# Delta rule in a fused two-block kernel: where the z columns stand, and where their gate meets the normed outputs

## The reference

```python
h = rms_norm(x, norm_mix[i])
proj = h @ w_in[i]
qkv_a, qkv_b, z_b, beta_b, alpha_b, gate_a, gate_b = split_columns(proj, IN_WIDTHS)
...                                   # windowed attention -> o_a (512 wide)
qkv_b = causal_short_conv(qkv_b, conv_w[i])
...                                   # q, k, v of 8 heads x 128
o_b = gated_delta_rule(qb, kb, vb, beta, g)
o_b = rms_norm(o_b, dn_out_norm[i]) * jax.nn.silu(z_b.reshape(b, s, DN_HEADS, DN_HEAD_DIM))
merged = (jax.nn.sigmoid(gate_a) * (o_a @ w_branch_a[i])
          + jax.nn.sigmoid(gate_b) * (o_b @ w_branch_b[i]))
x = x + merged @ w_out[i]
...                                   # mixture of experts, then a last gated path
```

## Time and profile before

| | us |
|---|---|
| median of three runs | 3188.21 (3187.32 to 3191.43) |
| the profiled execution, its own time | 3185.6 |
| its span | 3183.8 |
| TensorE busy | 2901.0 (91%) |
| VectorE busy | 1703.5 (54%) |
| ScalarE busy | 1253.5 (39%) |

### The profile page before, as it was taken

The page is one execution under the profiler, slowest core; times in us unless marked ns, Lnnn a source line. Parts: engine busy times, 40 slices in busy tenths (PEclk is TensorE's granted clock), DMA queues, the critical chain, the costliest instruction groups (busy, mean ns, idle before and its releaser), DMA issues.

```text
span 3183.8 us, 35407 instructions
## 1 busy us (share of the span) xinstructions
PE 2901.0 (91%) x13998; PEld 2293.4 (72%) x13998; DVE 1703.5 (54%) x2469; ACT 1253.5 (39%) x1913; POOL 14.8 (0%) x22
## 2 busy tenths in 40 slices
PE   6998899999999988999999999997778789969997
PEld 5566677888886656777888887775467677858886
DVE  4455535555334565355554335457575545459995
ACT  3233233333221442234332224454535434348883
POOL 0000000000000000000000000000000000000000
PEclk9999899999999989999999999998889899979998
DMA  4111113233331112122333321111110102259981
GB/s 161 47 40 62 42 39 98 94 99 98 93 124 61 44 47 60 34 78 93 98 99 112 100 93 59 61 60 40 40 47 29 44 28 86 94 209 369 394 336 54
DMA packets 96180, 307.70 MB, mean 97 GB/s; under 512 B 25744, under 2 KB 31760, under 8 KB 84240
## 3 DMA queue, kind: packets, MB, share of 16 engines
q1 hardware_dynamic: 69056, 284.88, 26.3%
q10 hardware_dynamic: 24368, 11.12, 1.2%
q0 software_dynamic: 2592, 9.44, 0.8%
HBM read 296.49 MB, written 8.91 MB: 96 GB/s over the span
## 4 chain that ended last, share of the span: by engine, by line
PE 78%; DVE 10%; ACT 6%; issue 4%; DMA 1%; ACTq 1%; POOL 0%; POOLq 0%; DVEq 0%
PE bank L370 19%; PE bank L372 18%; PE bank L371 18%; PE bank L365 2%; PE bank L367 2%; PE bank L366 2%; ACT flow_head L389 2%; DVE flow_rest L400 1%; PE bank L1929 1%; DVE dn L1812 1%; PE bank L2526 1%; PE bank L1232 1%; PE bank L1066 1%; PE bank L559 1%; PE bank L2011 0%
## 5 line engine op out<-in xcount | busy, mean ns | idle before, releaser
L400 DVE TENSOR_TENSOR flow_rest<-flow_raw,flow_head 128x1024 fp32r<-128x1024 f32 (+2 forms) x372 | 438.5, 1179 | 940.6 <-ACT flow_head L389 940.6
L370 PE MATMUL bank<-h_head,flow_head 128*128 128x512 f32 x2144 | 899.1, 419 | 28.5 <-DVE flow_rest L400 24.1
L371 PE MATMUL bank<-h_rest,flow_head 128*128 128x512 f32 x2144 | 847.3, 395 | 0.0
L372 PE MATMUL bank<-h_head,flow_rest 128*128 128x512 f32 x2144 | 846.6, 395 | 0.0
L389 ACT ACTIVATE flow_head<-flow_raw 128x1024 fp32r<-128x1024 f32 (+2 forms) x372 | 379.2, 1020 | 734.6 <-PE bank L372 686.6
L370 PEld LDWEIGHTS bank<-h_head,flow_head 128*128 128x128 f32 x2144 | 411.3, 192 | 148.2 <-issue 60.6
L371 PEld LDWEIGHTS bank<-h_rest,flow_head 128*128 128x128 f32 x2144 | 410.9, 192 | 91.9 <-issue 16.2
L372 PEld LDWEIGHTS bank<-h_head,flow_rest 128*128 128x128 f32 x2144 | 409.1, 191 | 88.7
L372 PE MATMUL bank<-ff_head,flow_rest 128*128 128x512 f32 x352 | 137.1, 390 | 0.0
L371 PE MATMUL bank<-ff_rest,flow_head 128*128 128x512 f32 x352 | 137.1, 389 | 0.0
L370 PE MATMUL bank<-ff_head,flow_head 128*128 128x512 f32 x352 | 137.1, 389 | 0.0
(11 more groups left out here) (607 smaller groups left out, 4218.4 us busy)
## 6 DMA issues: line engine op xcount, KB each, us to landing
flow_raw<-in_w_in SPq DMA_DIRECT2D x176, 512.0 KB, 3.5
ring<-in_experts SPq DMA_DIRECT2D x84, 1024.0 KB, 7.7
flow_raw<-in_w_gate_up SPq DMA_DIRECT2D x88, 512.0 KB, 3.4
flow_raw<-in_w_down SPq DMA_DIRECT2D x32, 512.0 KB, 3.5
flow_raw<-in_w_out SPq DMA_DIRECT2D x24, 512.0 KB, 3.5
flow_raw<-in_paths SPq DMA_DIRECT2D x24, 256.0 KB, 2.6
flow_raw<-in_w_down SPq DMA_DIRECT2D x16, 384.0 KB, 3.1
flow_raw<-in_path_b SPq DMA_DIRECT2D x8, 512.0 KB, 3.5
```

The lines of the kernel that those rows point to most:

```text
L370: nc.tensor.matmul(ps[u.bank][:, :], wh[:, c:c + P], head, start=start, stop=False)
L371: nc.tensor.matmul(ps[u.bank][:, :], wh[:, c:c + P], rest, start=False, stop=False)
L372: last = nc.tensor.matmul(ps[u.bank][:, :], wr[:, c:c + P], head, start=False, stop=stop)
L400: nc.vector.tensor_tensor(self.parts_of[p.slot][1][:, 0:p.words], p.raw, f32(self.parts_of[p.slot][0][:, 0:p.words]), ALU.subtract).then_i ...
```

## The change

The z units stand where they stood in the flow, between path A and path B, with the same weights and the same 64 ticks. What changes is what is written around them. `ends[5]`, the t1 of the delta rule's second half, is now the end of the z units plus 2 ticks. So that half's stages are spread over the 96 ticks of path A and the 64 of z, all its fractions unchanged. The z units use banks 6 and 7 alone, since the delta rule uses 4 and 5; they keep tanh-gated z in a buffer of their own (`k.zg`, 8 chunks, where path A's operands were). The product with the normed outputs, its head and its rest are a step of their own, `gated_outputs`, written behind the second half's last norm: 8 products (L1915), 8 heads (L1929), 8 rests (L1922), one chunk per tick from 3 ticks after the z units' end. The number and shape of instructions stay the same, but for table loads. From L1908 on, the lines of the changed kernel are other ones, those from `unit_norm` to `mixer_2` stand 20 lines later.

```diff
-    k.zt = at("zt", 40, (2, S))
+    k.zg = at("z_gate", 20, (DC, S))
...
-        o = k.x[c // PART][0][:, c % PART, :]
-
-        def keep(v, m, q=q):
-            return nc.vector.tensor_tensor(k.zt[:, q, :], k.ps[flow.units[m].bank][:, :], k.root[:, :], ALU.mult)
+        z = k.zg[:, c, :]
+
+        def keep(v, m, z=z):
+            return nc.vector.tensor_tensor(z, k.ps[flow.units[m].bank][:, :], k.root[:, :], ALU.mult)
...
-            k.dve_chain(nc.vector.scalar_tensor_tensor(k.zt[:, q, :], k.sgf2[:, q, :], 1.0, k.zt[:, q, :], ALU.add, ALU.mult))
+            nc.vector.scalar_tensor_tensor(z, k.sgf2[:, q, :], 1.0, z, ALU.add, ALU.mult).then_inc(*k.z_ready.up())
+
+        m = flow.unit(6 + c % 2, [(p, r * P) for r in range(DC)], operand(False), [(1, keep), (3, gate)], [(2, squash)])
+    return m
+
+
+def gated_outputs(k, chunks, t0):
+
+
+    nc, flow, v, a = k.nc, k.flow, k.v, k.a
+    base = chunks[0]
+
+    def vector_part():
+        for c in chunks:
+            flow.dve(t0 + c - base)
+            v.wait_ge(*k.z_ready.at(c + 1))
             v.wait_ge(*k.out_normed.at(c + 1))
-            nc.vector.tensor_tensor(k.zt[:, q, :], k.zt[:, q, :], o, ALU.mult).then_inc(*k.z_gated.up())
+            nc.vector.tensor_tensor(k.zg[:, c, :], k.zg[:, c, :], k.x[c // PART][0][:, c % PART, :], ALU.mult).then_inc(*k.z_gated.up())
+            if c > base:
+                rest(c - 1)
+        rest(chunks[-1])
+
+    def rest(c):
+        v.wait_ge(*k.z_heads.at(c + 1))
+        nc.vector.scalar_tensor_tensor(k.dr[:, c, :], k.zg[:, c, :], 0.5, f32(k.dh[:, c, :]), ALU.mult,
+                                       ALU.subtract).then_inc(*k.dn_split.up())
+
+    def scalar_part():
+        for c in chunks:
+            flow.act(t0 + c - base)
             a.wait_ge(*k.z_gated.at(c + 1))
...
-    flow.unit(4 + c % 4, [(p, r * P) for r in range(DC)], operand(False), [(1, keep), (3, gate), (6, rests)],
-                  [(2, squash), (4, heads)])
+            nc.scalar.activation(k.dh[:, c, :], k.zg[:, c, :], ACT.Copy, scale=0.5).then_inc(*k.z_heads.up())
...
-    z_units(k, dram)
+    k.z_end = z_units(k, dram)
...
-    ends.append(flow.units[k.path_a_end].end + 2)
+    ends.append(flow.units[k.z_end].end + 2)
...
+    gated_outputs(k, range(DC), ends[5] + 1)
```

More of the change, by code:

```diff
@@ L1885, in z_units, with squash @@
         p, q = flow.piece(dram["w_in_2"][Z_UNIT + c]), c % 2
-        o = k.x[c // PART][0][:, c % PART, :]
-        def keep(v, m, q=q):
-            return nc.vector.tensor_tensor(k.zt[:, q, :], k.ps[flow.units[m].bank][:, :], k.root[:, :], ALU.mult)
-        def squash(a, m, q=q):
+        z = k.zg[:, c, :]
+        def keep(v, m, z=z):
+            return nc.vector.tensor_tensor(z, k.ps[flow.units[m].bank][:, :], k.root[:, :], ALU.mult)
+        def squash(a, m, q=q, z=z):
             k.tables(EXP_TANH)
@@ L1893, in squash, with gate @@
             a.wait_ge(*flow.emptied_by(m))
-            nc.scalar.activation(k.sgf2[:, q, :], k.zt[:, q, :], ACT.Tanh, scale=0.5).then_inc(*k.z_squashed.up())
-        def gate(v, m, c=c, q=q, o=o):
+            nc.scalar.activation(k.sgf2[:, q, :], z, ACT.Tanh, scale=0.5).then_inc(*k.z_squashed.up())
+        def gate(v, m, c=c, q=q, z=z):
             v.wait_ge(*k.z_squashed.at(c + 1))
-            k.dve_chain(nc.vector.scalar_tensor_tensor(k.zt[:, q, :], k.sgf2[:, q, :], 1.0, k.zt[:, q, :], ALU.add, ALU.mult))
-            v.wait_ge(*k.out_normed.at(c + 1))
-            nc.vector.tensor_tensor(k.zt[:, q, :], k.zt[:, q, :], o, ALU.mult).then_inc(*k.z_gated.up())
@@ L1902, in heads @@
-        def heads(a, m, c=c, q=q):
-            a.wait_ge(*k.z_gated.at(c + 1))
-            nc.scalar.activation(k.dh[:, c, :], k.zt[:, q, :], ACT.Copy, scale=0.5).then_inc(*k.z_heads.up())
-        def rests(v, m, c=c, q=q):
-            v.wait_ge(*k.z_heads.at(c + 1))
-            nc.vector.scalar_tensor_tensor(k.dr[:, c, :], k.zt[:, q, :], 0.5, f32(k.dh[:, c, :]), ALU.mult,
-                                           ALU.subtract).then_inc(*k.dn_split.up())
-        flow.unit(4 + c % 4, [(p, r * P) for r in range(DC)], operand(False), [(1, keep), (3, gate), (6, rests)],
-                  [(2, squash), (4, heads)])
+            nc.vector.scalar_tensor_tensor(z, k.sgf2[:, q, :], 1.0, z, ALU.add, ALU.mult).then_inc(*k.z_ready.up())
@@ new lines, in z_units @@
+        m = flow.unit(6 + c % 2, [(p, r * P) for r in range(DC)], operand(False), [(1, keep), (3, gate)], [(2, squash)])
[7 more added lines that the diff above has]
+            v.wait_ge(*k.z_ready.at(c + 1))
+            v.wait_ge(*k.out_normed.at(c + 1))
+            nc.vector.tensor_tensor(k.zg[:, c, :], k.zg[:, c, :], k.x[c // PART][0][:, c % PART, :], ALU.mult).then_inc(*k.z_gated.up())
[9 more added lines that the diff above has]
+            flow.act(t0 + c - base)
+            a.wait_ge(*k.z_gated.at(c + 1))
+            nc.scalar.activation(k.dh[:, c, :], k.zg[:, c, :], ACT.Copy, scale=0.5).then_inc(*k.z_heads.up())
+    vector_part()
+    scalar_part()
@@ L3405, in stream @@
             "conv_tapped", "conv_convolved", "conv_squashed", "conv_done", "gates_squashed_2", "paths_added_2", "merged_heads_2",
-            "merged_rests_2", "z_squashed", "z_gated", "z_heads", "attn_split", "dn_split", "table_2_landed", "qk_done",
+            "merged_rests_2", "z_squashed", "z_ready", "z_gated", "z_heads", "attn_split", "dn_split", "table_2_landed", "qk_done",
             "win_done", "gates_ready", "dn_normed", "out_normed"))
```

2 lines of the change are left out of this document (1 added, 1 removed).

## The result

The changed kernel takes 3202.37 us (median of 7 runs, 3193.86 to 3205.41) against 3187.32 (7 runs, 3181.58 to 3194.48) of the kernel before: ratio 1.0041, 95% interval 1.0029 to 1.0054. By the ratio that is 13 us slower, with 9 and 17 as bounds; the two medians are 15 apart. The time lies in the forecast range of 3186 to 3205, 6 us above the forecast time and 2.6 under the range's upper end.

What follows compares the result with a forecast made beforehand. TensorE, busy for 91% of the span, was taken to bound the kernel, with its idle time in the second half open to filling. Terms 1.8 + 1.0 - 3.8 + 9.2 = 8.2 us slower than 3188.2 gave 3196.4; range 3186 to 3205.

Steps and rivals of the forecast that it cites:

- q and k norm: Second half's norm before the pairs: 8 more ticks, but last Ln 7.2 us later through four more loads; 1.8 us lost.
- pairs: Matmuls after the q and k norm: said to wait for nothing themselves, before or after the change.
- block solve: Solve ahead of the inverse: one wait becomes 3.6, 2.3 and 6.9 us; 1.0 us lost (0.3 gained to 2 lost).
- inverse, scan, output norm: Rest of the second half: shorter waits and less low clock, against one new wait; 3.8 us gained.
- new step: Gated outputs before path B: waits of 2.0 and 5.5 us, next piece late, low clock; 9.2 us lost.
- set 1: First set of the inverse: a rest stands ahead of an update, giving a new wait of 1.4 us.
- set 2: Second set of the inverse: 3 ticks instead of 1 cut 1.4 us off the wait of 3.0.
- low clock behind the 3.0: Slow matmuls after the wait before the inverse's second set: 1.8 us lost before the change, which should go.
- Rival 4: Much slower: every table load costs double in both norms, 8 more loads than before; 3207 us, chance 0.04.
- Rival 3: Faster: other engines' chains keep their length, so each wait is cut by all its new ticks; 3179 us, chance 0.09.

Runs made afterwards that it cites:

- tables_qk: Changed kernel with the Ln and Exp table set asked for by name only in the second half's q and k norm; 3189.17 us.
- early_norm: Changed kernel with the second half of the delta rule ending 24 ticks earlier, the gated products left where they were; 3209.84 us.
- head_first: Changed kernel with the second half's first eight block solve DMA issues written one tick later, behind the flow head; 3195.00 us.
- tables_end6: Changed kernel with table set asked for in all norms, block solve's DMA issues one tick later, half's end 6 ticks earlier, products unmoved; 3166.39 us.
- before_tables: Kernel before the change with the table set asked for ahead of every Ln and Exp of the norms; 3167.89 us.
- split: Changed kernel with chunks 0 to 3 of the gated outputs moved ahead of the output norm; 3206.87 us.
- tables_out: Changed kernel with the Ln and Exp table set asked for by name only in the second half's output norm; 3195.11 us.
- tables: Changed kernel with the table set asked for ahead of every Ln and Exp of the norms; 3169.98 us.
- end_alone: Changed kernel with the delta rule's second half spread over path A only, gated products still behind the z units; 3192.35 us.

## Why the prediction was right, and where its sizes were off

Milestones in both traces, counted from the half's first sum, give each term of the sum; one tick is 0.68. The last two rows are parted at path B's first tick.

| term | forecast | measured | how |
|---|---|---|---|
| q and k norm | 1.8 lost | 2.4 lost | pairs start at +31.09 (+23.22 before), less 8 ticks |
| pairs | 0 | 1.2 lost | their last matmuls end at +73.36 (+54.79), less 14 more ticks |
| block solve | 1.0 lost | 2.3 lost | from there to the transposes 34.02 (24.23), less 11 ticks |
| inverse, scan, output norm | 3.8 gained | 2.8 gained | the rest of the half |
| new step | 9.2 lost | 10.2 lost | from path B's first tick (+213.77, before +210.64) to the second mark 102.56 (92.39): waits of 1.92 and 5.21, low clock |
| sum | 8.2 | 13.3 | |

All five terms came out worse than forecast, so no error hid another. The sum was 5 us too small; it is the width of the range that held the result.

**The signs and the places were right, but for the pairs, put at nothing.** The wait before the pairs stayed in its stated range, at 5.74 with eight loads ahead of the last Ln (the forecast sum amounts to 7.5 there; the rest now stands in the wait of 1.66 inside the norm, which the forecast doesn't have); the solve shows 3.51, 2.34 and 6.01 for 3.6, 2.3 and 6.9; set 1 has the new 1.53 for 1.4, set 2 1.66 for 1.7, with 0.55 more behind it; path B 1.92 and 5.21 for 2.0 and 5.5. Such numbers can be had from a trace of the kernel before by walking through each engine's new order, one instruction after the other.

**What was too small is the clock's share behind each wait.** The forecast had 1.7 us at most behind the 3.6 in the solve and took 1.0 for the whole stage; measured are 14 matmuls at 0.43 instead of 0.23, 2.8 us. The chain carries it on: the second head of the solve, which needs TensorE 10 ticks on, was forecast 10.6 us after the end of the pairs and starts at 13.5, and VectorE's solving ends at 23.5 instead of 20.5. Behind the last wait it had 1.3 us, measured are 12 such matmuls, some 2.6 us with the first tick. Before the pairs it had nothing new, since the wait is as long as before; but the low clock lasted from 2497.49 to 2502.3 (4.8 us), where in the trace of before it lasted from 2493.99 to 2497.1, and that is most of the 1.2 of the pairs. Over the stretch the same matmuls kept TensorE busy for 6.1 us more, of the 13.3. (Of the low clock behind the 3.0 the forecast has 1.8 us; half of its own 3.2 is 1.6.)

**The loads were in the sum, but not weighed as its largest part.** The forecast had four more in each norm and let 5.1 us of them be covered by the 8 new ticks. The runs show what that cover was worth: without the loads those ticks would have emptied the wait before the pairs, as the missing wait in tables_qk shows, and with it the low clock. They were also priced a little low. With two loads a chunk takes 4.46 us from Ln to Ln (2482.84 to 2487.30), without 1.62 (2478.45 to 2480.07 in the trace of before): 1.42 for each load, since without a load an activation starts some 0.1 us before the one ahead of it ends. Four loads are 5.7 and not 5.1, and that is the 0.6 by which the norm's term was short. Rival 4, a load that costs double, falls: in the changed trace an Exp again starts 1.29 us after its load began (2484.07, 2485.36). The Trainium skill (ScalarE: Activation LUTs, "What ACT_TABLE_LOAD costs") has 2.66 us with the drain; the rows decide for 1.28 to 1.30 from the load's start to the next activation, and 1.42 in a chunk. The Trainium skill (ScalarE: Activation LUTs, "Table sets: the hidden batching unit") counts one load for an Ln and an Exp behind it, since one set holds both. The traces of before and of the changed kernel disagree, with two per chunk behind a tanh; tables_qk agrees, once the set is asked for by name.

**Rival 3** (faster by 9, the chains keep their length) had the right place for its gain, the waits, and the wrong premise. The chains are lengthened by the loads and by the heads and gates written into them (early_norm, head_first). Even without the loads the gain of tables_end6 over before_tables is 1.8 us between the marks.

What stays open: what sets the low clock behind a wait. Its length alone doesn't: behind the solve's wait of 3.5 it was low for 14 matmuls in three traces (changed, split, tables_out) and not at all in tables_qk, so the 2.8 us above belong to this order and aren't a price of such a wait. Open is also why the part ahead of the change differs by up to 6 us between profiled executions with the same instructions there (the first mark lies between 2466.4 and 2472.7 in the kernels without the table edit), and why the ratio of split (20 us) is larger than its stretch says (13.7).

## What to carry to other kernels

Idle time of an engine is worth filling only if the chain that causes it isn't lengthened by the filling. Write out, for each engine, which instructions of the filler come to stand inside that chain, above all in front of DMA issues, behind a wait, and between functions of different table sets. Leave room in a forecast for what the clock takes behind each wait: 2.6 to 2.8 us here behind waits of 3.5 and 5.2 in the changed kernel, and nothing behind one of 3.5 in another order. And look for the load that nobody asked for: two lines that name the table set took 18 us (14 to 23) off the kernel before and 29 off the changed one, more than the change that was being studied costs.

## What the runs showed of the hardware that was not expected

- In the changed kernel TensorE's next matmuls of 512 columns start 0.22 to 0.34 us apart behind waits of 1.66, 1.92 and 2.34 us; behind those of 3.51 and 5.21 us they start 0.43 apart, for 6.1 and 5.2 us (granted clock 0.50, its lower level, 1.2 GHz, against 2.4).
- The length of the wait doesn't decide it alone. In tables_qk the clock granted in the 6 us behind the same wait is 1.00, and the matmuls start 0.23 apart at once (rows below); in tables, behind 3.51 us, five start so and then seven 0.43 apart. Behind the 1.92 of end_alone eight start 0.43 apart, behind the same 1.92 of early_norm none.

```profile
2542.28 0.50 PE L370 MATMUL bank<-attn_head,flow_head 128*128 128x512 f32 x1 [3.52 <-DVE sgf L1842]
2542.62 0.40 PE L371 MATMUL bank<-attn_rest,flow_head 128*128 128x512 f32 x1
2542.85 0.39 PE L372 MATMUL bank<-attn_head,flow_rest 128*128 128x512 f32 x1
```

- With the same order ahead of it, it repeats: behind the wait before the pairs the low stretch lasted 3.1 us in both kernels whose half ends with path A (before and end_alone, wait 5.68), and 4.8 us in all four of the spread kernels with the loads there and this end (changed, head_first, split, tables_out, waits 5.71 to 5.75).
- A table load takes 1.28 us and costs 1.42 in a chunk of the norm. A set that is asked for by name costs one load at each change of function group; left to itself, each Ln and each Exp behind a tanh had its own: 12 loads against 4 between the marks in the norms of the changed and the former kernel, and with the edit 7 in all, tanh's included.
